# First out-projection of a hybrid trunk: own rows of blocks 4 and 5 ahead of the turns, and the last head's loads in another order

## What is computed

```python
for l in range(2):
    h  = modulate(rmsnorm(x), shift1, scale1)          # latent; hc likewise for context in layer 0
    y  = hgrn2(h, hc)  if l == 0 else short_conv(h)    # mixer, ends in a product with w_out
    x  = x + g1 * rmsnorm(y)
    hf = modulate(rmsnorm(x), shift2, scale2)
    x  = x + g2 * rmsnorm(swiglu(hf))                  # FFN, hidden width 2816
```

## Time and profile before

| what | us |
|---|---|
| runs, median of 3 | 2582.47 |
| the profiled execution's own time | 2578.82 |
| its span | 2577.1 |
| PE busy | 2497.1 (97%) |
| DVE busy | 1865.2 (72%) |
| GpSimd busy | 1299.2 (50%) |
| ACT busy | 1155.0 (45%) |
| mean granted PE clock | 0.992 |

### The profile page before, as it was taken

One profiled execution on the slowest core, in us unless ns is written; L12 is line 12 of the kernel. 1 busy time (PEld: TensorE's weight loads), 2 busy tenths in 40 slices (PEclk: granted clock), 3 DMA queues, 4 the chain that ended last, 5 costly groups with the idle time before them and its releaser, 6 DMA issues.

```text
span 2577.1 us, 35639 instructions
## 1 busy us (share of the span) xinstructions
PE 2497.1 (97%) x12324; PEld 2087.5 (81%) x12324; DVE 1865.2 (72%) x2445; ACT 1155.0 (45%) x2157; POOL 1299.2 (50%) x859
## 2 busy tenths in 40 slices
PE   7999999999999889999999999999999999999998
PEld 5888888888887778888888877887887888888886
DVE  5377778767866577888877988888656565556888
ACT  5334534444443553333334467433454334334544
POOL 3121321432330047777767972688214767766983
PEclk9999999999999999999999999999999999999999
DMA  6223432432352333444458342132523322345533
GB/s 263 70 72 130 180 118 87 156 128 72 128 225 103 147 131 111 158 152 156 157 196 305 115 123 86 46 118 99 196 75 130 121 98 88 122 171 217 188 101 112
DMA packets 124249, 351.12 MB, mean 136 GB/s; under 512 B 12753, under 2 KB 12753, under 8 KB 121041
## 3 DMA queue, kind: packets, MB, share of 16 engines
q1 hardware_dynamic: 124112, 349.33, 38.4%
HBM read 258.58 MB, written 90.70 MB: 136 GB/s over the span
## 4 chain that ended last, share of the span: by engine, by line
PE 79%; DVE 9%; POOL 3%; issue 3%; ACT 3%; DMA 2%; SPq 1%; DVEq 0%; ACTq 0%; POOLq 0%
PE psum L1552 18%; PE psum L1554 18%; PE psum L1553 18%; PE psum L2155 4%; PE psum L2156 4%; PE psum L2157 4%; PE psum L1812 2%; PE psum L1814 2%; PE psum L1813 2%; PE psum L1764 2%; POOL row_unit_sum L1468 2%; PE psum L1751 1%; PE psum L1778 1%; PE psum L1734 1%; DVE k_all L3394 1%
## 5 line engine op out<-in xcount | busy, mean ns | idle before, releaser
L1552 PE MATMUL psum<-x_hi,unit 128*128 128x512 f32 x1232 | 485.1, 394 | 12.5 <-DVE x_lo L3048 11.9
L1553 PE MATMUL psum<-x_lo,unit 128*128 128x512 f32 x1232 | 481.3, 391 | 0.0
L1554 PE MATMUL psum<-x_hi,unit 128*128 128x512 f32 x1232 | 481.1, 391 | 0.0
L3048 DVE TENSOR_TENSOR c_set<-c_set,psum 128x512 f32<-128x512 f32 x352 | 233.2, 684 | 222.3 <-ACT c_set L2282 144.8
L1417 POOL TENSOR_TENSOR unit<-unit_sum,unit 128x512 fp32r<-128x512 f32 x200 | 290.5, 1461 | 17.5 <-ACT unit L2282 15.6
L1552 PEld LDWEIGHTS psum<-x_hi,unit 128*128 128x128 f32 x1232 | 232.4, 189 | 68.7 <-ACT c_set L2282 10.0
L1554 PEld LDWEIGHTS psum<-x_hi,unit 128*128 128x128 f32 x1232 | 232.3, 189 | 48.8
L1553 PEld LDWEIGHTS psum<-x_lo,unit 128*128 128x128 f32 x1232 | 232.3, 189 | 47.3
L1552 PE MATMUL psum<-h_hi,w_hi 128*128 128x512 f32 x624 | 262.7, 421 | 1.8 <-DVE h_lo L3048 1.8
L1554 PE MATMUL psum<-h_hi,w_lo 128*128 128x512 f32 x624 | 244.2, 391 | 0.0
L2155 PE MATMUL psum<-row_unit_hi,part_hi 128*128 128x512 f32 x616 | 241.3, 392 | 3.0 <-DVE part_lo L3048 1.8
(11 more groups left out here) (355 smaller groups left out, 5781.4 us busy)
## 6 DMA issues: line engine op xcount, KB each, us to landing
ffn_raw<-in_w_ffn_in SPq DMA_DIRECT2D x80, 512.0 KB, 6.0
part_raw<-parts_kept SPq DMA_DIRECT2D x154, 256.0 KB, 2.7
parts_kept<-part_sums SPq DMA_DIRECT2D x22, 1280.0 KB, 5.5
ada_half<-in_ada SPq DMA_DIRECT2D x96, 256.0 KB, 2.6
out_raw<-in_w_ffn_out SPq DMA_DIRECT2D x44, 512.0 KB, 7.9
w_raw<-in_w_hgrn_in SPq DMA_DIRECT2D x40, 512.0 KB, 3.6
ada_raw<-in_ada SPq DMA_DIRECT2D x32, 512.0 KB, 4.8
units_kept<-stage_unit SPq DMA_DIRECT2D x28, 512.0 KB, 2.9
```

What stands on the lines that cost most here:

```text
L1552: begin = pe.matmul(out_ap, hi[:, a:b], rhs_hi, start=first, stop=False)
L1553: pe.matmul(out_ap, hi[:, a:b], rhs_lo, start=False, stop=False)
L1554: return begin, pe.matmul(out_ap, lo[:, a:b], rhs_hi, start=False, stop=last)
L3048: V.tensor_tensor(dst, a, b, op).then_inc(S[sem], 1)
```

## The change

PE: in `fill` the wait for evacuations is taken per bank; after the 28 slots, block 4 is made with kb outermost in two banks (14 slots, two copies awaited at its start, each mix awaited by its own semaphore); `head` takes eight slots more ahead of the near products, five per level instead of six, and none behind the levels; `first_projection` has own rows 4 and 5 earlier and one slot of block 7 less. ACT: copies 4 and 5 ahead of level 5; block 5's square behind the turned parts 2 and 3; the turned rows of block 7 ahead of the last high and of the first two copies of the FFN. DVE: block 7's M3 sum ahead of block 6's M3 low. SP: the two stores of staged units go behind row 6, the first halves of mixes 0 and 1 to the end; the second halves of mixes 2 to 5 count on the semaphores `raw_loaded0` to `raw_loaded3`, whose later waits are raised by 32.

```diff
@@ -406,7 +406,7 @@
 
 
 def raws_loaded(f, slot):
-    return f * (PAIR_LOADS + 16 * len(range(slot // 2, CONV_PAIRS, 2)))
+    return 32 + f * (PAIR_LOADS + 16 * len(range(slot // 2, CONV_PAIRS, 2)))
 
 
 def pick(t, i):
@@ -758,7 +758,7 @@
             return tuple(part[:, :, :] for part in conv_parts[kind][:2])
 
         def conv_raw_after(p, slot):
-            return PAIR_LOADS + 16 * (p // 2 + 1)
+            return 32 + PAIR_LOADS + 16 * (p // 2 + 1)
 
         def raw_slots(u):
 
@@ -1054,15 +1054,17 @@
                              ).then_inc(S[f"stage_loaded{m}"], 16)
             for r in range(1, 3):
                 row_load(r)
-            stage_stores(HEADS - 1, C_SPOT)
             sp.wait_ge(S["ada_step"], 8 * HEADS)
             row_load(3)
             sp.wait_ge(S["mix_stored"], 32 * SPLIT_MIXES)
             sp.wait_ge(S["gemm_full"], O_CONV)
-            for m in (*range(FIRST_MIXES, SPLIT_MIXES), *range(FIRST_MIXES)):
+            def mix_load(m):
                 for part in range(2):
                     sp.dma_start(as_f32(mix_halves[0][part][0][:, m, :]), mix_kept[m, part]
                                  ).then_inc(S[f"kept_loaded{m}"], 16)
+
+            for m in range(FIRST_MIXES, SPLIT_MIXES):
+                mix_load(m)
                 if m == 3:
                     row_load(4)
             sp.wait_ge(S["sigmoids"], 4 * HEADS)
@@ -1071,10 +1073,13 @@
                 sp.wait_ge(scan_sem[d], (HEADS - 1) * SCAN_STEPS + 1)
             sp.wait_ge(S["gs_ready"], HEADS)
             row_load(6)
+            stage_stores(HEADS - 1, C_SPOT)
             for m in range(SPLIT_MIXES):
                 for part in range(2):
                     sp.dma_start(as_f32(mix_halves[0][part][1][:, m, :]), mix_kept[m, 2 + part]
-                                 ).then_inc(S["mix_late"], 16)
+                                 ).then_inc(S["mix_late" if m < FIRST_MIXES else f"raw_loaded{m - FIRST_MIXES}"], 16)
+            for m in range(FIRST_MIXES):
+                mix_load(m)
             sp.wait_ge(S["scan_full"], HEADS * SCAN_USES + U_LEVEL)
             sp.dma_start(last_row_raw[:, :], w_hgrn_out[KB - 1]).then_inc(S["row_loaded7"], 16)
 
@@ -1869,15 +1874,15 @@
                 own_row(2)
                 take(seventh, 4)
                 own_row(3)
-                take(seventh, 4)
+                take(seventh, 3)
                 pe.wait_ge(S["proj_evac"], 2)
+                take(sixth, 1)
+                own_row(4)
                 take(sixth, 2)
                 turn_parts(0, 0, 1)
-                own_row(4)
+                own_row(5)
                 turn_parts(0, 2, 3)
-                take(sixth, 2)
-                own_row(5)
-                take(sixth, 3)
+                take(sixth, 4)
                 turn_parts(1, 0, 1)
                 take(sixth, 2)
                 turn_parts(1, 2, 3)
@@ -1905,7 +1910,6 @@
 
             def fill():
 
-                pe.wait_ge(S["gemm_evac"], 4 + O_CONV)
                 for kb in range(KB - 1):
                     pe.wait_ge(S[f"row_loaded{kb}"], 16)
                     if kb < FIRST_MIXES:
@@ -1916,6 +1920,8 @@
                         pe.wait_ge(S["mix_split"], late_mix(kb, 0))
                     for tb in (2, 3):
                         for c in range(2):
+                            if kb == 0:
+                                pe.wait_ge(S["gemm_evac"], 4 + O_CONV + min(2 * (tb % 2) + c - 3, 0))
                             begin, mm = rows_products(0, bank(2 * (tb % 2) + c), hgrn_rows[kb], c, kb, tb,
                                                       kb == 0, kb == KB - 2, first_mix[kb] if kb < FIRST_MIXES else None)
                             if tb == 2 and c == 0:
@@ -1924,12 +1930,21 @@
                                 mm.then_inc(S["part_full"], 1)
                             yield
                 out_rows(0, 6)
-                for i, (tb, c) in enumerate(PARTS[4:] + [(0, 0), (0, 1), (1, 0), (1, 1)]):
-                    pe.wait_ge(S["part_evac"], i + 1)
-                    if tb >= 4:
-                        pe.wait_ge(S["mix_late"], 32 * SPLIT_MIXES)
+                pe.wait_ge(S["part_evac"], 2)
+                pe.wait_ge(S["mix_late"], 32 * FIRST_MIXES)
+                for kb in range(KB - 1):
+                    if kb == KB - 2:
                         pe.wait_ge(S["mix_split"], late_mix(KB - 2, 1))
-                    else:
+                    elif kb >= FIRST_MIXES:
+                        pe.wait_ge(S[f"raw_loaded{kb - FIRST_MIXES}"], 32)
+                    for c in range(2):
+                        _, mm = rows_products(0, bank(c), hgrn_rows[kb], c, kb, 4, kb == 0, kb == KB - 2)
+                        if kb == KB - 2:
+                            mm.then_inc(S["part_full"], 1)
+                        yield
+                for i, (tb, c) in enumerate(PARTS[6:] + [(0, 0), (0, 1), (1, 0), (1, 1)]):
+                    pe.wait_ge(S["part_evac"], i + 3)
+                    if tb < 4:
                         for m in range(FIRST_MIXES):
                             pe.wait_ge(S[f"kept_loaded{m}"], 32)
                     for kb in range(KB - 1):
@@ -2007,15 +2022,14 @@
                     for part in range(3):
                         v_transposes(hs, part)
                         slots(1)
-                    slots(19)
+                    slots(27)
                     for part in range(2):
                         for _ in near(hs, part, True):
                             slots(1)
                     for i in FAR_LEVELS:
                         for part in range(2):
                             level(hs, i, part)
-                            slots(3)
-                    slots(3)
+                            slots(2 + part)
                     for d in (FWD, BWD):
                         for part in range(3):
                             key_transposes(hs, d, part)
@@ -2625,9 +2639,11 @@
                                     max(unit_stored(3, j) for j in range(slot, PRODUCTS, 3)))
                     for i in range(4):
                         part_out(i)
-                    for i in (3, 4, 5):
+                    for i in FAR_LEVELS:
+                        if i == 5:
+                            part_out(4)
+                            part_out(5)
                         merge_level(i)
-                    merge_level(6)
                 if hg is not None and hs is not None:
                     evacuate(0, 0, cols(z[FWD], 0, CTX))
                     evacuate(0, 1, cols(z[FWD], 1, CTX))
@@ -2663,8 +2679,6 @@
                         stage_highs(hg, A_SPOT)
                     if hg is None:
                         out_row_copy(0)
-                        for i in (4, 5):
-                            part_out(i)
                     for part in range(3):
                         key_tokens(FWD, part)
                     if hg is None:
@@ -2746,8 +2760,8 @@
                 y_square(4)
                 turned_parts(0, 0, 1)
                 x_square(3)
+                turned_parts(0, 2, 3)
                 y_square(5)
-                turned_parts(0, 2, 3)
                 x_high(0, M2, 0)
                 x_square(4)
                 turned_parts(1, 0, 1)
@@ -2766,6 +2780,7 @@
                 turned_raw(1, LAT - 2)
                 x_high(0, M3, 4)
                 x_high(0, M5, 6)
+                turned_raw(1, LAT - 1)
                 x_high(0, M3, 6)
 
             def projection(sub, inst):
@@ -2813,7 +2828,8 @@
 
                 act.sem_inc(S["unit_hi"], 2 * PRODUCTS)
                 copy_m2(0, 0)
-                turned_raw(inst, LAT - 1)
+                if f == 1:
+                    turned_raw(inst, LAT - 1)
                 if f == 0:
                     act.wait_ge(S["kept1"], 32)
                 copy_m4(0, 1)
@@ -3180,7 +3196,9 @@
                 x_sums(0, 4, IN_TIME)
                 x_lows(0, 4, IN_TIME)
                 x_sums(0, 6, IN_TIME)
-                x_lows(0, 6, IN_TIME)
+                x_lows(0, 6, (M5,))
+                x_sums(0, LAT - 1, (M3,))
+                x_lows(0, 6, (M3,))
 
             def projection(sub, inst):
                 f = sub // 2
@@ -3606,7 +3624,8 @@
                     hidden_part(u, h, e, 1)
 
                 add(0, 1, 1)
-                x_sums(f, LAT - 1, (M3,))
+                if f == 1:
+                    x_sums(f, LAT - 1, (M3,))
                 x_lows(f, LAT - 1, (M5, M3))
                 for kind in (M1, M7):
                     for b in LATE_UNITS[f]:
```

## The result

The changed kernel takes 2564.28 us in the median (2560.63 to 2564.63, six runs) against 2582.30 us for the kernel before, run beside it: ratio 0.9928, 95% interval 0.9915 to 0.9941, 18.0 us faster. The forecast was 2566.2 (2560 to 2574). In a later set of runs the ratio was 0.9926 (0.9914 to 0.9938).

The account below looks back on a forecast made before the run. TensorE, busy 97% of the span, was taken as the bound, losing time in waits and low clock. Gains of 5.3 (head), 9.4 (out-projection) and 1.6 (FFN start) sum to 16.3 us: 2582.47 to 2566.2 us, range 2560 to 2574.

Parts of the forecast that it names:

- The forecast's case: Whole kernel: the prediction's own main case, a time of 2562 to 2569 us, chance 0.52.
- Part A: Last scan head: per-bank waits, reordered loads and moved slots and copies bring the keys' transposes 5.3 us earlier.
- Part B: Out-projection: own rows 4 and 5 earlier remove waits before turns and slow matmuls, gain 9.4 us (bounds 5 and 10.5).
- part C: FFN start: block 7's turned rows and M3 sum earlier shorten the 6.57 us M3 wait, gain 1.6 us.
- one slot more: Last head: one more slot of three matmuls runs before the keys' transposes, costing 0.7 us, given back in the out-projection.
- two waits of 1.0 us are left: Last head: PE still waits 1.0 us each for mix 2 and row 5, replacing the 3.23 us wait.
- The late mixes: Last head: mixes 0 and 1, loaded last, and the late stores delay the near products by 0.2 us (bounds 0 and 8).
- the two gains: Last head: 3.6 us from per-bank waits and 2.6 us from the load order, simply added.
- The chain: Out-projection: own row 4, DVE's addition, ACT's square and copies, then block 3's diag come early enough for PE's turns.
- No half gain: Denies the rival that ACT or the loads take half the gain: 2569 to 2570.5 us, chance 0.22.
- no clock that falls at every load: Last head: denies that DMA waits between short groups of matmuls return PE to half rate at every group, chance 0.05.
- Slower: Last head: rival that the clock stays low throughout, 36 slots costing 21 us, giving 2586 us, chance 0.05.

Follow-up runs that it names:

- the run again: The unchanged changed kernel measured once more in a later set beside the kernel before: 2560.35 us against 2581.31, ratio 0.9926.
- the old loads: Changed kernel with SP's old order, stores ahead of row 3 and mixes 0 and 1 ahead of row 5: 2569.28 us, 0.9958 to the kernel before.
- one wait: Changed kernel with one wait for the last evacuation of g ahead of all of fill, new load order kept: 2566.79 us, 0.9946 to the kernel before.
- the kernel without the third part: Changed kernel with ACT's turned rows and DVE's M3 sum for block 7 back at their old places: 2563.17 us, 0.9928 to the kernel before.
- the three others that lack it: Kernel before (2582.30 us), and that kernel with only the head's edits (2574.03 us, 0.9974) or only the out-projection's (2571.32 us, 0.9965).

## Why the prediction was right

**The sum.** Forecast 16.3 us, measured 18.0. The forecast's case held, and parts A and B came out at their places and a little larger; part C brought less than its term, so the whole lies nearer than A and B do.

**Part A, 5.3 forecast, 7.0 measured (8.7 in the run again).** The mechanisms stood: g's wait 0.53 us (0.66 forecast), no slow matmuls, mix 2 and row 5 landing 9.0 and 18.0 us after the adaLN sums (9.05 and 18.15 forecast, 766.2 and 775.3 less 757.15), one slot more. The term that was mis-sized is "two waits of 1.0 us are left": 0.49 and 0.55 us in one execution, none in another. Two small terms were on the safe side too: the levels lost nothing where I had taken 0.3, and PE's idle 0.35 us at 790.97 before the levels, which I had not counted, went. PE's 0.33 us wait for the copies of blocks 4 and 5 went, as forecast. The late mixes took 0.49 us (0.2 forecast). The sum took the two gains as independent. With the old loads the banks and the rest bring 2.4 us, because 1.6 us more than before are waited at the loads; with the new loads and one wait the head gains 3.5 (100.20 - 96.71); together they bring 7.0 to 8.7. So what the banks bring hangs on the loads. That the whole is more than the sum of the two is not shown: each is one execution, and slow matmuls that happened to last longer took 1.3 us from the one with one wait.

**Part B, 9.4 forecast, 10.4 measured.** The chain ran as written. On the changed kernel's scale (7.51 us earlier, 857.35 to 849.84) the forecast has the addition of block 4 at 864.8, ACT's square at 866.0 and block 3's diag at 873.3; DVE's rows, then ACT's:

```profile
864.71 1.21 DVE L3064 TENSOR_TENSOR raw_b<-raw_b,psum 128x1024 f32<-128x1024 f32 x1
...
873.01 0.29 DVE L3115 TENSOR_SCALAR diag<-ident,x_rstd 128x128 f32<-128x128 f32 x1
```

```profile
865.96 1.06 ACT L2296 ACTIVATE junk_proj<-raw_b 128x1024 f32<-128x1024 f32 x1
```

The wait at the second pair's later turns is 0.37 us instead of 0.7, and the slow stretches of before had reached a little beyond the turns that I counted (the slot behind the first of them began with a 0.77 us matmul). The diag has little to spare: PE begins the turns that need it at 873.36. The 0.75 us wait before the last turns stayed, as forecast.

**Part C, 1.6 forecast, 0.4 to 1.4 measured.** The M3 wait is 4.66 us ("near 5 us" forecast) and M3 comes 1.92 us sooner, so the chain up to M3 stood. What failed is the step from there to the time: the forecast took M3's gain as the end's and put a later wait for DVE at nothing. M7 now waits 0.93 us, 31.2 us after the first FFN product, and what is left at the 14th product is 0.38 us against the kernel without the third part, and 0.8 to 1.4 us against the three others that lack it: from M3 to the next product it took 4.28 us in the former and 4.99 to 5.26 in these, and with no wait at M7 that counts in full. DVE's line of sums and lows, lengthened by GpSimd, sets M7's start. The cause that I gave for the long lows, GpSimd, is shown.

**The rivals.** No half gain (the loads came as early as the line says), no clock that falls at every load: waits of 0.5 us left it at 1.00 (774.65:778.00). The Trainium skill (TensorE: Matmul & The Clock Gate, HAM oscillation) tells of half rate behind each wait for DMA between short groups, in an example with waits of 3 to 5 us; the runs here agree for waits for DMA of 2.39 and 3.18 us, while 0.5 us left the clock at 1.00. In the rival *Slower* the last sum is a little off: 21 us of loss less the 16.3 gives 2587, not 2586, which changes nothing in it.

## What to carry to other kernels

Measure a chain of engines in starts relative to a start upstream of the change, and not in whole times alone: here the out-projection and the starts of M3 and M7 repeat to a few hundredths of a microsecond where two medians of the changed kernel differ by 3.9 us. Repeat the stage that hangs on loads: the head, measured the same way, moved by 1.7 us. When a wait is shortened, look for the next place where the engine that ended it will be late again (here DVE's lows for M7): what is gained ahead of that place counts only until PE has to wait there. Two removals that feed the same wait, early banks and early loads, are to be sized together: of what the banks gave alone, 1.6 us was waited away again at the loads.

## What was not expected

- M7 starts 31.21 to 31.24 us after the first FFN product in six executions with an M3 wait of 4.7 us, though the stretch of slow matmuls behind that wait differs among them (M3 to the next product took 4.41 to 5.26 us): the M7 wait is 1.45 and 1.47 us where it was short, 0.31 and 0.33 where it was long. A slow clock ahead of such a wait cost nothing here.
- The fall of the clock can come late: behind 2.73 us the first matmul is slow, behind 2.39 us the third (779.61), behind 3.18 us only the sixth (772.60). Behind the waits of 1.57, 1.61, 1.63 and 1.75 us the matmuls were not slow.
- How long slow matmuls last varies for the same wait: behind 2.73 us for g it was 3.1 us before and about 5.9 us in the kernel with one wait.
